# Relative position bias: from identity products on TensorE to an addition inside VectorE's row maximum

## The reference

```
s = einsum('bqhmd,bkhmd->bhmqk', q, k2) * QK_HEAD_DIM ** -0.5      # m = 0, 1: two score maps per head
dist = qpos - kpos
bias = rel_bias[t5_bucket(dist)]                                   # 32 buckets, per head
s = where(dist >= 0, s + bias, -1e30)
p = softmax(s)
o = (p[:, :, 0] - lam * p[:, :, 1]) @ v                            # then per-head RMSNorm
```

## Time and profile before

| | |
|---|---|
| median of 3 runs | 1419.58 us (1418.56 to 1420.76) |
| the profiled execution | 1421.63 us, span 1419.9 us |
| TensorE products | 1380.1 us busy, 97% |
| TensorE weight loads | 1243.1 us, 88% |
| VectorE, ScalarE, GpSimd | 708.6, 463.8, 170.0 us |
| TensorE's granted clock, mean | 0.991 of full speed |

### The profile page before, as it was taken

The page is one execution under the profiler, slowest core; times in us unless marked ns, Lnnn a source line. Parts: engine busy times, 40 slices in busy tenths (PEclk is TensorE's granted clock), DMA queues, the critical chain, the costliest instruction groups (busy, mean ns, idle before and its releaser), DMA issues.

```text
span 1419.9 us, 22498 instructions
## 1 busy us (share of the span) xinstructions
PE 1380.1 (97%) x8774; PEld 1243.1 (88%) x8774; DVE 708.6 (50%) x1091; ACT 463.8 (33%) x779; POOL 170.0 (12%) x321
## 2 busy tenths in 40 slices
PE   7999999989999899999999999999999999999996
PEld 6999999957667588899898989898989898989995
DVE  6333421165757555455636454545454545453647
ACT  5421021055646634334231313232323232323233
POOL 2253000021222121120000000000000000000005
PEclk9999999999999999999999999999999999999998
DMA  7112023165664514132110111111010202020107
GB/s 259 61 30 64 30 83 88 60 198 165 186 192 158 186 65 149 67 97 75 30 60 30 59 30 49 40 36 53 23 65 15 73 15 74 15 74 15 45 16 145
DMA packets 93289, 112.65 MB, mean 79 GB/s; under 512 B 6428, under 2 KB 65221, under 8 KB 93221
## 3 DMA queue, kind: packets, MB, share of 16 engines
q1 hardware_dynamic: 89845, 103.60, 23.2%
q0 software_dynamic: 1136, 4.06, 1.6%
q10 hardware_dynamic: 2240, 4.06, 0.8%
HBM read 96.76 MB, written 14.69 MB: 78 GB/s over the span
## 4 chain that ended last, share of the span: by engine, by line
PE 87%; DVE 4%; ACT 3%; issue 3%; POOL 2%; DMA 1%; ACTq 0%; DVEq 0%; POOLq 0%
PE PS L2131 36%; PE PS L2195 17%; PE PS L1863 16%; PE PS L2086 7%; PE PS L1956 2%; PE PS L1924 1%; PE PS L1979 1%; POOL small L1248 1%; PE PS L2025 1%; PE PS L1931 1%; DVE small L1438 1%; PE PS L2002 1%; PE PS L1946 1%; PE PS L1849 1%; DMA x_in<-in_x_prompt_dram 1%
## 5 line engine op out<-in xcount | busy, mean ns | idle before, releaser
L2131 PE MATMUL PS<-act_lo,wu_hi 128*128 128x364 f32 (+1 forms) x1056 | 346.6, 328 | 0.0
L2131 PE MATMUL PS<-act_hi,wu_hi 128*128 128x364 f32 (+1 forms) x1056 | 346.2, 328 | 0.2 <-DVE wu_lo L1691 0.2
L2131 PE MATMUL PS<-act_hi,wu_lo 128*128 128x364 f32 (+1 forms) x1056 | 346.2, 328 | 0.0
L2131 PEld LDWEIGHTS PS<-act_hi,wu_hi 128*128 128x128 f32 x1056 | 198.7, 188 | 1.1 <-DVE wu_lo L1691 0.5
L2131 PEld LDWEIGHTS PS<-act_lo,wu_hi 128*128 128x128 f32 x1056 | 198.3, 188 | 0.5
L2131 PEld LDWEIGHTS PS<-act_hi,wu_lo 128*128 128x128 f32 x1056 | 198.5, 188 | 0.0
L1677 DVE TENSOR_TENSOR y_acc<-y_acc,PS 128x512 f32<-128x512 f32 x180 | 123.5, 686 | 128.9 <-PE PS L2195 128.9
L2195 PE MATMUL PS<-wd_hi,g_hi 128*128 128x512 f32 x360 | 144.7, 402 | 0.0
L2195 PE MATMUL PS<-wd_lo,g_hi 128*128 128x512 f32 x360 | 142.3, 395 | 0.0
L2195 PE MATMUL PS<-wd_hi,g_lo 128*128 128x512 f32 x320 | 126.7, 396 | 0.0
L1132 ACT CAST g_hi<-conv 128x1088 fp32r<-128x1088 f32 x21 | 23.1, 1102 | 262.3 <-PE PS L2195 210.9
(11 more groups left out here) (257 smaller groups left out, 2343.9 us busy)
## 6 DMA issues: line engine op xcount, KB each, us to landing
wu_raw<-in_w_up_dram SPq DMA_DIRECT2D x44, 512.0 KB, 3.9
kpage<-in_cache_k_dram SPq DMA_DIRECT2D x64, 256.0 KB, 3.0
vpage<-in_cache_v_dram SPq DMA_DIRECT2D x64, 256.0 KB, 3.0
wd_raw<-in_w_down_dram SPq DMA_DIRECT2D x22, 512.0 KB, 5.2
w_raw<-in_w_in_dram SPq DMA_DIRECT2D x20, 512.0 KB, 4.7
wo_raw<-in_w_out_dram SPq DMA_DIRECT2D x8, 512.0 KB, 5.5
x_res<-in_x_prompt_dram SPq DMA_DIRECT2D x8, 512.0 KB, 4.1
out_dram<-x_mid SPq DMA_DIRECT2D x8, 512.0 KB, 2.9
```

The costliest lines, as they stand in the source:

```text
L2131: mm = nc.tensor.matmul(PS[:, 3 * half + c, 0:kept(c)], a[:, half, k, :], b[:, k, KEPT[c]], start=(j == 0), stop=(j == len(parts) - 1))
```

## The change

The four bias products of each step, `identr`, and the split of the table into two parts go. Queries are scaled by the negative of 1/sqrt(d), and the table is negated when it is taken out of PSUM, so PSUM holds negated scores. `row_max` becomes: for steps wider than two blocks a minimum over the far columns into `far_min`, a wait for it on the same engine, and one operation over the last 256 columns (128 for w = 1) that adds the bias, writes the sums back to PSUM, and takes the minimum of them and of `far_min`. The exponent reads with scale -1. The samples follow in sign. TensorE's `scores` counts each map when its last product is done. SP waits for the last maximum instead of the last score.

```diff
-    identr = keep.put("identr", [P, P], F32R)
+    far_min = keep.put("far_min", [P, 4, 2])
...
-    bias_raw = bias.put("bias_raw", [P, H, 2 * P])
-    bias_hi = bias.put("bias_hi", [P, H, 2 * P], F32R)
-    bias_lo = bias.put("bias_lo", [P, H, 2 * P], F32R)
-    qp = at("qp", BIAS, [P, NB, H, 32])
+    qp = bias.put("qp", [P, NB, H, 32])
+    bias_sb = bias.put("bias_sb", [P, H, 2 * P])
...
+    def far_count(i, m):
+        return sum(2 for j in range(i) if width(j) > 2) + m + 1
... SP
-        sp.wait_ge(score_ready, 2 * NSTEP)
+        sp.wait_ge(nmax_ready, 2 * NSTEP)
         load_w_out(range(6, KD))
... ScalarE
-        act.wait_ge(bias_loaded, 16)
-        nc.scalar.copy(bias_hi[:], bias_raw[:]).then_inc(bias_hi_ready, 1)
...
-        nc.scalar.copy(sq[:], qT[:, :, 0:NS]).then_inc(sqk_ready, 1)
+        nc.scalar.activation(sq[:], qT[:, :, 0:NS], ACT.Copy, scale=-1.0).then_inc(sqk_ready, 1)
...
-            nc.scalar.activation(dst, score_cols(i, m), ACT.Exp, bias=nmax[:, i % 4, m:m + 1],
+            nc.scalar.activation(dst, score_cols(i, m), ACT.Exp, scale=-1.0, bias=nmax[:, i % 4, m:m + 1],
... GpSimd
-        pool.wait_ge(const_ready, 3)
-        nc.gpsimd.tensor_copy(identr[:], ident[:]).then_inc(const_ready, 1)
...
-        pool.wait_ge(bias_lo_ready, 1)
+        pool.wait_ge(gate_mul, STEPS)
         nc.gpsimd.memset(qp[:], 0.0).then_inc(qp_zero, 1)
-        pool.wait_ge(gate_mul, STEPS)
... VectorE
-            nc.vector.tensor_copy(line_out[:, h, :], PS[:, 4 + h, 0:LINE]).then_inc(line_taken, 1)
+            nc.vector.tensor_scalar(line_out[:, h, :], PS[:, 4 + h, 0:LINE], -1.0, None, ALU.mult).then_inc(line_taken, 1)
...
-                    nc.vector.tensor_scalar(dst, PS[:, bank_of[n], 0:w], DH ** -0.5, None, ALU.mult).then_inc(dve_took, 1)
+                    nc.vector.tensor_scalar(dst, PS[:, bank_of[n], 0:w], -DH ** -0.5, None, ALU.mult).then_inc(dve_took, 1)
...
-                if c == 0 and half == 1:
-                    dve.wait_ge(bias_hi_ready, 1)
-                    nc.vector.tensor_tensor(bias_lo[:], bias_raw[:], bias_hi[:].bitcast(F32),
-                                            ALU.subtract).then_inc(bias_lo_ready, 1)
...
         def row_max(i, m):
+            h, w = i // QB, P * width(i)
+            far = max(0, w - 2 * P)
             dve.wait_ge(score_ready, 2 * i + m + 1)
-            nc.vector.tensor_reduce(nmax[:, i % 4, m:m + 1], score_cols(i, m), AX.X, ALU.max, negate=True).then_inc(nmax_ready, 1)
+            if far:
+                nc.vector.tensor_reduce(far_min[:, i % 4, m:m + 1], score_cols(i, m)[:, 0:far], AX.X, ALU.min).then_inc(far_ready, 1)
+                dve.wait_ge(far_ready, far_count(i, m))
+            near = score_cols(i, m)[:, far:w]
+            nc.vector.tensor_tensor_reduce(near, near, bias_sb[:, h, 2 * P - (w - far):2 * P], 1.0,
+                                           far_min[:, i % 4, m:m + 1] if far else -NEG, ALU.add, ALU.min,
+                                           accum_out=nmax[:, i % 4, m:m + 1]).then_inc(nmax_ready, 1)
... TensorE, scores(i)
-            if i == 0:
-                pe.wait_ge(bias_lo_ready, 1)
...
             for c, e in parts:
-                biased = max(c, b0)
                 for m in range(2):
                     d = slice(DH * m, DH * m + DH)
-                    nc.tensor.matmul(score_cols(i, m)[:, c:e], qT[d, h, qs], kT[d, h, NS + c:NS + e], start=True, stop=biased >= e)
-            for m in range(2):
-                for c, e in parts:
-                    biased = max(c, b0)
-                    if biased < e:
-                        t = slice(biased - (w - 2 * P), e - (w - 2 * P))
-                        for j, b in enumerate((bias_hi, bias_lo)):
-                            mm = nc.tensor.matmul(score_cols(i, m)[:, biased:e], identr[:], b[:, h, t], start=False, stop=(j == 1))
-                mm.then_inc(score_ready, 1)
+                    mm = nc.tensor.matmul(score_cols(i, m)[:, c:e], qT[d, h, qs], kT[d, h, NS + c:NS + e], start=True, stop=True)
+                    if e == w:
+                        mm.then_inc(score_ready, 1)
```

More of the change, by code:

```diff
@@ L141, in _program @@
     ident = keep.put("ident", [P, P])
-    identr = keep.put("identr", [P, P], F32R)
+    far_min = keep.put("far_min", [P, 4, 2])
+    keep.put("spare", [P, P - 8])
     gain = keep.put("gain", [P, D])
@@ L370, in _program @@
     bias_loaded = sem("bias_loaded")
-    bias_hi_ready = sem("bias_hi_ready")
-    bias_lo_ready = sem("bias_lo_ready")
+    far_ready = sem("far_ready")
     score_ready = sem("score_ready")
@@ L708, in _ @@
         skewed = bass.AP(toeplitz, P - 1, [[LINE - 1, P], [P * LINE, H], [1, 2 * P]])
-        sp.dma_start(bias_raw[:], skewed).then_inc(bias_loaded, 16)
+        sp.dma_start(bias_sb[:], skewed).then_inc(bias_loaded, 16)
         sp.dma_start(pages[:], page_table.rearrange("b n -> (b n)").rearrange("(a n) -> a n", a=1)).then_inc(page_loaded, 16)
@@ L1196, in _ @@
         nc.gpsimd.memset(small[:], -0.5).then_inc(const_ready, 1)
-        nc.gpsimd.memset(smp_bias[:], NEG).then_inc(sbias_zero, 1)
+        nc.gpsimd.memset(smp_bias[:], -NEG).then_inc(sbias_zero, 1)
         nc.gpsimd.memset(ws_bd[:], 0.0).then_inc(bd_zero, 1)
@@ L1485, in own_softmax @@
                 nc.vector.tensor_tensor(own[:, pr, :], PS[:, PV_BANK, NS * pr:NS * pr + NS], smp_bias[:, c0:c0 + NS],
-                                        ALU.add).then_inc(own_biased, 1)
+                                        ALU.subtract).then_inc(own_biased, 1)
             dve.wait_ge(own_biased, NB // 2)
@@ L1494, in smp_softmax @@
                 last_page = PS[:, SMP_BANK, 384:512]
-                nc.vector.tensor_tensor(last_page, last_page, smp_bias[:, 0:P], ALU.add).then_inc(dve_step, 1)
+                nc.vector.tensor_tensor(last_page, last_page, smp_bias[:, 0:P], ALU.subtract).then_inc(dve_step, 1)
                 own_step(dve, dve_step)
@@ L1557, in _ @@
         dve.wait_ge(lam_ready, 1)
+        dve.wait_ge(bias_loaded, 16)
         for i in range(NSTEP):
@@ L1819, in _ @@
     def _(pe):
-        pe.wait_ge(const_ready, 4)
+        pe.wait_ge(const_ready, 3)
         def bias_lines(heads):
@@ L1906, in scores @@
             w = P * n
-            b0 = max(0, w - 2 * P)
-            if i == 0:
-                pe.wait_ge(bias_lo_ready, 1)
             if i >= 1:
```

## The result

The changed kernel takes 1423.34 us (median of 20 runs, 1420.73 to 1427.52), the kernel before 1420.01 (20 runs, 1418.16 to 1422.49). The ratio is 1.0025, with a 95% interval of 1.0017 to 1.0034: 3.3 us slower, inside the forecast range. It lies 1.6 us above the forecast itself, 0.4 of which is that the kernel before came out at 1420.01 here and at 1419.58 in the runs that the forecast started from. The profiled execution took 1422.4 us, its span 1420.7, the mean clock 0.993.

What follows compares the result with a forecast made beforehand. In the attention stage engines take turns: wide steps are a loop without TensorE, narrow steps follow it. Saving 7.4 us and paying 28 times 0.34 us on VectorE's maxima gives +2.1 on 1419.6, so 1421.7 us; range 1415 to 1431.

Steps and rivals of the forecast that it cites:

- Wide steps are a loop without TensorE; removing products gives nothing there.: Steps of 5 to 7 blocks: maxima, exponents, square, GpSimd's power and `out_norm` set the period; bias products run beside, saving nothing.
- 2x per wide transition: Between wide steps both lengthened maxima are on the path; three transitions per head, 12 in all, together 24x.
- x: Time each row maximum on VectorE gets longer: 0.34 us taken, 28 times on the path; break-even at 0.26.
- T: Duration of VectorE's new operation over the near 256 columns: 0.58 us taken, including half of a 0.20 hand-over.
- The saving of 7.4 us: TensorE's removed bias products, 0.57 us per step, on the path mainly at w = 2 to 4, plus w = 5 of head 3.
- w = 8 of heads 0 to 2 and w = 1 at nothing: Widest and narrowest steps gain nothing, as TensorE waits for `out_norm`; at w = 8 up to 0.5 us of price hides.
- w = 4 of heads 1 and 2: the saving, less x: Steps of 4 blocks save 0.57 us of bias products but pay for the second maximum, alone on the path.
- The rest at nothing: `bias_lo`, `bias_hi`, the `identr` cast, sign changes, `memset(qp)` and SP's w_out load: no change of time.
- Rival 1 (TensorE bounds): TensorE bounds the attention stage, so 13.7 us come back, 1406 us; chance 0.13.
- rival 2 (operation as short as an addition): VectorE's new operation costs like a plain addition: -2.4 to -0.7 us, 1417 to 1419; chance 0.17.
- rival 3 (half rate): VectorE's new operation is long; at half rate +11.9 us, 1431, or 1435 with the full hand-over; chance 0.11.
- Rival 4 (the clock falls more often): TensorE's share sinks at w = 4 and 5, bringing half clock: +4 us on top of the forecast, 1426; chance 0.11.

Runs made afterwards that it cites:

- p1: The kernel before without its 128 bias products on TensorE, so prompt scores get neither bias nor mask: 1414.59 us, ratio 0.9962.
- p2: The changed kernel with four products of zeros per step, of the old shapes, put back on TensorE: 1428.53 us, ratio 1.0062.
- look_after_1: The changed kernel, not edited, profiled once more: 1420.83 us, span 1419.1.
- look_after_2: The changed kernel, not edited, a further profiled execution: 1425.68 us, span 1424.0.
- p6: The changed kernel with `out_norm` behind the first maximum in steps 5 to 7 blocks wide of heads 0 to 2: 1420.19 us, ratio 0.9999.
- q1: The kernel before with `out_norm` behind the first maximum in steps 5 to 7 blocks wide of heads 0 to 2: 1422.8 us, ratio 1.002.
- p4: The changed kernel, but steps of 5 blocks and wider get the bias by float32 identity products and a plain minimum: 1421.26 us, ratio 1.0009.
- p5: The changed kernel with `out_norm` later in steps 5 to 7 blocks wide of heads 0 to 2, float32 bias products in head 3's first two steps: 1418.39 us.

## Why the prediction came out right

The direction, the mechanism and the range were right; two terms were off, in opposite directions.

- *Wide steps are a loop without TensorE; removing products gives nothing there.* Right: p1 left those of heads 0 to 2 within 0.02 us.
- *2x per wide transition.* Right in kind: 0.54 to 0.60 in heads 0 to 2. Not in all of head 3: at w = 5, where VectorE had waited 0.48 for the scores, the longer maxima used up that wait; p1, p2 and the change all stand at -0.39 to -0.41 there, and w = 6 paid 0.33 in place of 2x. The forecast had booked the saving and all 24x.
- *The size of x.* Mis-sized: 0.34 taken. The nine wide steps of the change, 5.15 us for 18x, give 0.29; p2's median, 8.6/28, gives 0.31 (0.25 to 0.38 by its interval). T was 0.55, not 0.58: pointer as taken, hand-over 142 ns, of which 0.06 lies behind the recorded end. The forecast's 28 x 0.34 = 9.5 was 0.9 too high. (The Trainium skill, "VectorE: DVE Perf Modes", section Two Vector instructions with no wait between them, had an operation with an accumulator as two instructions. The rows of the kernel after show the pair 64 times.)
- *The saving of 7.4 us.* Mis-sized, and by more: p1 measured 5.4 (3.7 to 7.2). The failed step is "0.5 + 2 x 0.57 = 1.65" for head 0; p1 shows 0.75 there, of which w = 2 and 3 aren't firm. Firm is w = 4: 0.57 was taken, 0.03 came, since another engine is late. In the timeline of the kernel after, the last four key transposes wait for ScalarE's copy `at_sb`, which stands behind four small exponents for the samples (L950) and doesn't depend on the products (p1 has the same wait, 0.28 us, at 303.43):

```profile
303.26 0.65 PE L1970 MATMUL PS<-ident,kpage 128*128 128x128 f32 x4 [0.23 <-ACT at_sb L931]
```

Heads 1 and 2 gave 1.57 each (1.7 taken), as a step gives 0.51 to 0.53, not 0.57. In head 3, w = 8, 7 and 6 gained 0.3 in sum where nothing was booked. The firm steps together gave 4.9 where 5.6 was booked; the rest of the 2.0 us lies in the start of the stage and in the clock, and no run separates it.
- *w = 8 of heads 0 to 2 and w = 1 at nothing.* Right: 0.00 and +0.04. `turn_out` waits for `out_norm` as it did: it starts at 326.50, when `out_norm`, started at 326.09, is done; the line is

```profile
326.50 0.66 PE L1961 MATMUL PS<-ident,o_nrm 128*128 128x128 f32 x4 [0.72 <-DVE o_nrm L1458]
```
- *w = 4 of heads 1 and 2: the saving, less x.* -0.57 + 0.34 = -0.23 by the forecast, -0.21 measured, -0.53 in p1, +0.32 in p2. Whether w = 3 of head 0 pays its x isn't shown: p2 has -0.10 there, but that mark isn't firm.
- *The rest at nothing.* No step shows it; the first mark moved by 0.16, less than two executions of one kernel differ there (0.99 between look_after_1 and look_after_2), and 560 us to the end is unchanged.
- *Rival 1 (TensorE bounds)* fell with p1, *rival 2 (operation as short as an addition)* with 493 + 142 ns, *rival 3 (half rate)* with 493 ns.
- *Rival 4 (the clock falls more often)* is true in part. Not where it was put: over 404 to 408 us TensorE's share did sink to 2.67 of 4 us, but the clock stayed at 1.00. What low stretches there are lie at the start of the stage, at w = 3 of head 3 and behind the stage, in either kernel. Whether they come, and how long they last, differs by execution.

What stays open: the firm steps sum to +2.9 us, the medians differ by 3.3, and the steps that aren't firm put the sum anywhere from +2.0 to +3.5 by the pair of traces that is compared (w = 3 of head 3 left out). So nothing has to be missing. The changed kernel may meet low-clock stretches more often, which would fit its wider spread of times (6.8 us against 4.3 over 20 runs each) and its mean granted clock, 0.9926 over these 20 runs against 0.9938 over 61 runs of the kernel before. But p6 has 0.9919 over 11 runs and takes no longer than before, so this isn't shown.

So, by the medians, the two errors, 2.0 us of saving too much and 0.9 of price too much, left 1.1 us of the 1.2 by which the change (+3.3 for +2.1) was forecast too low. It was right by its mechanism, but its closeness is in part luck. So is the clear sign: with its own saving of 7.4 and the measured x of 0.29 the sum would have been 28 x 0.29 - 7.4 = +0.7 us, no difference that could be told from none.

## What to carry to other kernels

In a stage where engines take turns, list the steps and ask of each what its first late wait is; the same edit may be worth its full length in one step, nothing in the next, and its opposite in a third. Compare the same work for it, from the end of the w = 4 step of head 0 to the end of the last step. Work taken off an engine that is busy 94% of the stage gave four tenths of its length: in p1 TensorE is busy 11.8 us less (169.2 to 157.4), and the stretch is 4.5 us shorter (177.1 to 172.6). Work added to one that is busy 63% was paid by three quarters, as most of it stood inside the loop: in p2 VectorE is busy 10.9 us more (113.4 to 124.2), and the stretch is 8.0 us longer, 1.2 of which is the clock at w = 3 of head 3. Once such a move is made, the order of the other engine's queue is to be chosen anew: here the order that took the price of the change away (p6) was worse than useless without the change (q1).

## What the runs showed of the hardware beyond that

- A VectorE operation with an accumulator over 256 columns in PSUM: 428 ns with a constant, 493 with a column pointer, then a hand-over of 142 ns that overlaps its end. With the column pointer it is 0.55 us from the start to the end of the hand-over, and ScalarE's exponent started at 0.59. For 128 columns the operation takes 296 ns.
- Executions of one kernel, equal within 0.02 us in each step from w = 4 of head 0 to w = 4 of head 3, differed by up to 4.9 us (look_after_1 and look_after_2). 3.5 us of it lie in two places where the lower clock level was granted in one and not, or half as long, in the other; 1.3 lie at the start of the stage, under the same mean clock. The place in the middle of the stage lies where TensorE had just waited 1.02 us, but p4 and p5 have the same wait and no low stretch. A step-by-step comparison of marks resolves a few hundredths, outside of these places, where the total resolves 1 us.
